# First pair of output tiles of both SwiGLU stages computed from features before the division by the deviation

## What is computed

```
def rms_norm(x, g):
    xf = x.astype(jnp.float32)
    y = xf * lax.rsqrt(jnp.mean(xf * xf, axis=-1, keepdims=True) + EPS)
    return (y * g.astype(jnp.float32)).astype(x.dtype)

def modulate(h, shift, scale):
    return h * (1 + scale) + shift

def swiglu(h, w1, w3, w2):
    return (jax.nn.silu(h @ w1) * (h @ w3)) @ w2

        # first_block, in each of the two layers:
        h = h + g1 * y
        hn = modulate(rms_norm(h, norm_ffn_g[layer]), sh2, sc2)
        h = h + g2 * swiglu(hn, ffn_w1[layer], ffn_w3[layer], ffn_w2[layer])
```

## Time and profile before

| | us |
|---|---|
| three runs, median | 1212.85 |
| three runs, lowest and highest | 1206.35 and 1214.12 |
| span of the profiled execution | 1207.4 |
| TensorE busy in it | 1149.0 (95%) |
| VectorE busy | 814.4 (67%) |
| ScalarE busy | 589.9 (49%) |
| GpSimd busy | 81.8 (7%) |

### The profile page before, as it was taken

How to read it: one execution, slowest core, us unless ns; L and a number is a source line. 1 busy time by engine, 2 the same in 40 slices (tenths; PEclk the granted TensorE clock), 3 DMA queues, 4 the chain that set the end, 5 groups by cost and what they waited for, 6 DMA issues and landing times.

```text
span 1207.4 us, 24317 instructions
## 1 busy us (share of the span) xinstructions
PE 1149.0 (95%) x10429; PEld 1092.4 (90%) x10429; DVE 814.4 (67%) x1490; ACT 589.9 (49%) x1084; POOL 81.8 (7%) x100
## 2 busy tenths in 40 slices
PE   5888789999998999999989999999999999999999
PEld 2687689999997999999989888888999999999999
DVE  3783668898886767555674678787664665877543
ACT  2434556454544545454465557653234445655432
POOL 0000110000011000001100111112600001000000
PEclk9789999999999999999998999999999999999999
DMA  9751548889884555751653232232123464855520
GB/s 388 291 207 60 215 170 329 334 340 349 320 328 174 222 222 223 255 187 43 246 175 105 106 105 80 97 105 71 38 72 106 157 211 159 323 198 185 208 84 14
DMA packets 32363, 226.41 MB, mean 188 GB/s; under 512 B 3584, under 2 KB 4736, under 8 KB 5120
## 3 DMA queue, kind: packets, MB, share of 16 engines
q1 hardware_dynamic: 30528, 221.20, 49.1%
q10 hardware_dynamic: 1728, 3.67, 0.8%
HBM read 223.80 MB, written 1.05 MB: 186 GB/s over the span
## 4 chain that ended last, share of the span: by engine, by line
PE 86%; DVE 8%; ACT 4%; DMA 1%; issue 1%; POOL 0%; SPq 0%; DVEq 0%; POOLq 0%
PE bank L562 23%; PE bank L563 22%; PE bank L564 22%; PE bank L1041 2%; PE bank L687 2%; DVE sb_tmp L1915 1%; DVE sb_ring L1930 1%; DVE sb_wlo L1889 1%; PE bank L580 1%; PE bank L1032 1%; PE bank L1063 1%; DMA sb_ring<-in_ada 1%; PE bank L590 1%; PE bank L600 1%; PE bank L1229 1%; PE bank L1247 1%
## 5 line engine op out<-in xcount | busy, mean ns | idle before, releaser
L562 PE MATMUL bank<-sb_xh,sb_whi 128*128 128x256 f32 x1488 | 422.9, 284 | 9.0 <-DVE sb_wlo L1889 6.7
L563 PE MATMUL bank<-sb_xl,sb_whi 128*128 128x256 f32 x1488 | 414.3, 278 | 0.0
L564 PE MATMUL bank<-sb_xh,sb_wlo 128*128 128x256 f32 x1488 | 414.3, 278 | 0.0
L1889 DVE TENSOR_TENSOR sb_wlo<-sb_ring,sb_whi 128x1024 fp32r<-128x1024 f32 (+1 forms) x197 | 239.1, 1220 | 138.5 <-ACT sb_whi L1375 138.1
L562 PEld LDWEIGHTS bank<-sb_xh,sb_whi 128*128 128x128 f32 x1488 | 281.6, 189 | 17.6 <-issue 12.8
L563 PEld LDWEIGHTS bank<-sb_xl,sb_whi 128*128 128x128 f32 x1488 | 282.2, 190 | 0.1
L564 PEld LDWEIGHTS bank<-sb_xh,sb_wlo 128*128 128x128 f32 x1488 | 281.7, 189 | 0.0
L1375 ACT ACTIVATE sb_whi<-sb_ring 128x1024 fp32r<-128x1024 f32 (+1 forms) x197 | 206.7, 1053 | 88.7 <-PE bank L564 81.3
L1889 DVE TENSOR_TENSOR sb_wlo<-sb_more,sb_whi 128x1024 fp32r<-128x1024 f32 x108 | 131.0, 1222 | 64.8 <-ACT sb_whi L1375 64.8
L562 PE MATMUL bank<-sb_hh,sb_whi 128*128 128x256 f32 x608 | 168.4, 277 | 0.0
L564 PE MATMUL bank<-sb_hh,sb_wlo 128*128 128x256 f32 x608 | 167.8, 276 | 0.0
(11 more groups left out here) (378 smaller groups left out, 1845.6 us busy)
## 6 DMA issues: line engine op xcount, KB each, us to landing
sb_more<-in_w SPq DMA_DIRECT2D x34, 1024.0 KB, 6.7
sb_ring<-in_w SPq DMA_DIRECT2D x32, 1024.0 KB, 6.0
sb_ring<-in_adaT SPq DMA_DIRECT2D x26, 1024.0 KB, 7.6
sb_ring<-in_f SPq DMA_DIRECT2D x22, 1024.0 KB, 5.0
sb_more<-in_adaT SPq DMA_DIRECT2D x18, 1024.0 KB, 9.5
sb_ring<-in_gn SPq DMA_DIRECT2D x8, 1024.0 KB, 4.9
sb_ring<-in_gd SPq DMA_DIRECT2D x8, 1024.0 KB, 4.9
sb_ring<-in_up SPq DMA_DIRECT2D x8, 1024.0 KB, 5.9
```

Of the source, the lines that this page charges most:

```text
L562: te.matmul(out, wh, rh, start=start, stop=False, skip_group_check=skip)
L563: te.matmul(out, wh, rl, start=False, stop=False, skip_group_check=skip)
L564: return te.matmul(out, wl, rh, start=False, stop=stop, skip_group_check=skip)
L1889: ve.tensor_tensor(lo, x, hi.bitcast(F32), ALU.subtract).then_inc(*lo_dve.up(n))
```

## The change

For pair 0 of both layers the product no longer starts from the finished `xh` and `xl`. With r the factor of a token (one over the deviation), the input of SwiGLU is (h times scale) times r plus shift. So the weights' product with it is r times (weights times h times scale), plus weights times shift. `gh` and `gl` hold the high and low parts of h times scale for 256 tokens, and of the shift as columns 257 and 258 (twice the same, which makes the width even). ScalarE writes `gh` behind each square, VectorE writes `gl` behind each residual, one tile later. TensorE's `unnormed` runs pair 0 on them in two banks; the sums of squares stand after feature tile 1 of it, the spreading of the factor after tile 4, and the idle matmuls are left out. Pair 1 then runs as `opening` did before. ScalarE copies the spread factor to SBUF after `upper`, VectorE multiplies both outlets by it and copies out the shift's column, the Silu takes it as bias, and a last operation of VectorE adds the other shift's product and multiplies.

```
-                idle(2)
+                idle(2 * (norm not in ("ffn0", "ffn1")))
...
-                idle(2 * (norm not in ("mix0", "ctx", "fin")))
+                idle(2 * (norm not in ("mix0", "ctx", "fin", "ffn0", "ffn1")))
...
+            def unnormed(layer, norm, outs):
+
+                us = [F.take(f"w13_{layer}")[0] for _ in outs]
+                for u in us:
+                    P.wait_ge(*lo_done(u))
+                P.wait_ge(*dve.at("gl", norm, "shift"))
+                for k in range(KT):
+                    c = slice(k * 128, (k + 1) * 128)
+                    P.wait_ge(*act.at("gh", norm, k))
+                    for u, out in zip(us, outs):
+                        _, hi, lo = unit_of(u)
+                        te.matmul(out, hi[:, c], gh[:, k, :], start=k == 0, stop=False)
+                        te.matmul(out, lo[:, c], gh[:, k, :], start=False, stop=False)
+                    P.wait_ge(*dve.at("gl", norm, k))
+                    for e, (u, out) in enumerate(zip(us, outs)):
+                        _, hi, _ = unit_of(u)
+                        end = te.matmul(out, hi[:, c], gl[:, k, :], start=False, stop=k == KT - 1)
+                        if k == KT - 1:
+                            end.then_inc(*pe.up(("up", layer, 0, e), ("unit", u)))
+                    if k == 1:
+                        mean_square_rest(norm)
+                    if k == 4:
+                        spread(norm)
+                for u in us:
+                    F.done(u)
...
                 for j in range(NH0):
-                    ps = take(RG, ("up", layer, j), (dve, ("prod", layer, j)))
                     if j == 0:
-                        opening(f"w13_{layer}", norm, [(ps[:, 0:T], True), (ps[:, T:2 * T], False)], [("up", layer, 0, e) for e in range(2)])
-                    for e in range(2 if j else 0):
+                        unnormed(layer, norm, [take(RG, ("up0", layer, e), (dve, ("up0", layer, e)))[:, 0:T + 2] for e in range(2)])
+                    else:
+                        ps = take(RG, ("up", layer, j), (dve, ("prod", layer, j)))
+                    if j == 1:
+                        opening(f"w13_{layer}", norm, [(ps[:, 0:T], True), (ps[:, T:2 * T], False)], [("up", layer, 1, e) for e in range(2)])
+                    for e in range(2 if j > 1 else 0):
...
+            def upper_scaled(norm, i, j):
+
+                A.wait_ge(*dve.at("h", norm, j))
+                A.wait_ge(*dve.at("scl", i))
+                sc.activation(gh[:, j, 0:T], h[:, j, :], ACT.Copy, scale=scl[:, i, j:j + 1]).then_inc(*act.up(("gh", norm, j)))
...
                 upper(norm, mods[:, layer, 24:32], xh, free)
+                sc.activation(sq[:, 1, :], ps_of(("spread", norm))[:, 0:T], ACT.Copy).then_inc(*act.up(("R", norm)))
...
+                    if j == 0:
+                        A.wait_ge(*dve.at("up0", layer, 0))
+                        sc.activation(r, sq[:, 2, :], ACT.Silu, bias=st[:, 0:1]).then_inc(*act.up(("silu", layer, j)))
...
+            def lower_scaled(norm, i, j):
+
+                V.wait_ge(*act.at("gh", norm, j))
+                V.wait_ge(*dve.at("h", norm, j))
+                ve.scalar_tensor_tensor(gl[:, j, 0:T], h[:, j, :], scl[:, i, j:j + 1], gh[:, j, 0:T].bitcast(F32),
+                                        ALU.mult, ALU.subtract).then_inc(*dve.up(("gl", norm, j)))
...
             m2 = dve.now()
+            V.wait_ge(*m2)
+            scaled(2, C("nf", 0, 8), mods[:, 0, 32:40])
+            dve.note(("scl", 2))
+            lower_shift(0, "ffn0")
...
                 residual("ffn0", j, "mo", mods[:, 0, 16 + j:17 + j])
+                if j > 0:
+                    lower_scaled("ffn0", 2, j - 1)
                 if j == 6:
                     split(ahead)
+            lower_scaled("ffn0", 2, 7)
...
+                    if j == 0:
+                        V.wait_ge(*act.at("R", norm))
+                        for e in range(2):
+                            ps = ps_of(("up0", layer, e))
+                            V.wait_ge(*pe.at("up", layer, 0, e))
+                            ve.tensor_copy(st[:, e:e + 1], ps[:, T:T + 1]).then_inc(*dve.up())
+                            ve.tensor_tensor(sq[:, 2 + e, :], ps[:, 0:T], sq[:, 1, :], ALU.mult).then_inc(*dve.up(("up0", layer, e)))
+                        V.wait_ge(*dve.now())
+                        V.wait_ge(*act.at("silu", layer, 0))
+                        ve.scalar_tensor_tensor(r, sq[:, 3, :], st[:, 1:2], r, ALU.add, ALU.mult).then_inc(*dve.up(("prod", layer, 0)))
```

46 lines of the change are left out of this document (33 added, 13 removed).

## The result

| | before | changed |
|---|---|---|
| median of 6 runs each, on the same chip, us | 1211.51 | 1221.61 |
| lowest and highest, us | 1206.35 to 1214.85 | 1217.78 to 1222.14 |
| span of the profiled execution, us | 1207.4 | 1218.6 |

The ratio is 1.0099, 95% interval 1.0079 to 1.0119: the change makes the kernel 1.0% slower, 12 us of 1211.5 (9.6 to 14.4). The ratio is the recorded estimate and not the quotient of the medians in the table; those differ by 10.1, which lies inside the interval too. The forecast was 1222, a loss of 9.35, and the change is just at the 1% that was named as what a measurement can tell.

What follows compares the result with a forecast made beforehand. TensorE's chain bounds the kernel, with VectorE's `apply` and two splits setting the pace ahead of pair 1. Terms 0.4 + 2.95 + 1.6 + 2 x 2.2 = 9.35 on 1212.85 give 1222 us, range 1214 to 1230.

Steps and rivals of the forecast that it cites:

- The gap ahead of pair 1: TensorE waits for U2's and U3's `wlo`, split behind `apply`: 7.5 us in layer 0, 7.2 in layer 1.
- The clock: Behind each gap ahead of pair 1, 22 matmuls run at granted clock 0.50, costing 2.2 us a layer.
- the clock stays up: Rival: no half clock behind the gaps ahead of pair 1, so 1218 us; chance 0.12.
- down for all of pair 1: Rival: all of pair 1 runs at half clock, 2 x 2.6 us more, 1227; chance 0.08.
- The rival of 1243: Pair 0's wider matmuls run at the full float32 rate, 20.6 us more; chance 0.05.
- So `wlo` moves from 180.08 to 180.43: Layer 0, ahead of pair 0: one `gh` of 0.35 us on ScalarE delays U1's `wlo`.
- Layer 1: Pair 0 starts at the pooling's end, 389.86; pair 1 ends 1.6 us later, plus 2.2 for the clock.
- The wait ahead of the mixer: Layer 0: two small VectorE operations before `mixout`'s first split add 0.4 us (0.3 to 0.6) to TensorE's 3.12.
- tips over: Rival: the wait ahead of the mixer reaches 3.5, the clock falls, another 2.2 us, 1224.5; chance 0.13.
- The signs that were named: Changed profile: early pair 0, `apply` about 2 us later in layer 0 only, 7 to 8 us gaps, then half clock.
- What costs nothing: `gl` during `mixout`, pair 0's longer outlet and later next units are covered; without that cover 1 to 2 us.
- faster: Rival: both `wlo` come before or inside `apply`, so pair 1 doesn't wait: -9.6 us, 1203; chance 0.05.

Runs made afterwards that it cites:

- e1: Changed kernel with the splits of U2 and U3 moved ahead of `apply` in both layers; 1209.23 us, ratio 1.0010.
- e4: Kernel before, with the splits of U2 and U3 moved ahead of `apply`; 1209.56 us, ratio 1.0005.
- e2: Changed kernel with 14 idle matmuls on TensorE between pair 0 and pair 1 in both layers; 1216.94 us, ratio 1.0062.
- e3: Changed kernel with the small scale and shift operations moved from ahead of the mixer's splits to behind them; 1222.49 us, ratio 1.0094.
- e8: Changed kernel with the spreading behind feature tile 2 of pair 0 in place of tile 4; 1219.43 us, ratio 1.0097.
- e11: Changed kernel with ScalarE writing `gh` of a tile behind the next unit's rounding during `mixout`; 1219.02 us, ratio 1.0083.
- e5: e1 with the spreading behind tile 3 and the small operations moved as in e3; 1207.60 us, ratio 0.9990.
- e7: e5 with pair 0's outlet ahead of the next split and layer 0's adaLN tiles one pair later; 1203.29 us, ratio 0.9959.
- e12: e7 with `gh` written behind the next rounding as in e11; 1203.04 us, ratio 0.9938.

## Why the prediction held, point by point

The time (1222 forecast, 1221.61 measured) and the range held. The median of before was 1211.5 in the runs beside it and not 1212.85, so the loss was 12 (9.6 to 14.4; 10.1 between the medians) where I had 9.35. The hit to 0.4 us is luck in part: a base that was 1.3 too high made up for a loss that was too small. What was missing from my sum are two paces, 1.6 to 1.8 us in layer 0 and 1.2 in layer 1, both below; 9.35 and 2.9 make about 12.3. The two stages of the profiles lose 14.0, more than that, since the profile of before happens to have the full clock at the mixer's start and behind the wait for `z`, where the changed kernel's has half clock at both (about 0.8 each).

**The gap ahead of pair 1** is the heart of it, and it held to a tenth: 7.20 us for 7.5 in layer 0 and 6.88 for 7.2 in layer 1, both ended by a `wlo`. From the spreading to `apply` I had 0.65, and the rows have 187.33 - 186.68 = 0.65; from `apply` to pair 1 I had 9.3, and they have 196.63 - 187.33 = 9.30. e1 took the two splits out from behind `apply`, and the loss of 1% was gone; e4 showed that the same edit is worth nothing in the kernel before. This cause is shown.

**The clock** behind the gaps was 2.2 a layer in my sum; e2 measured 2.25 and 2.24. At 0.50 ran 24 matmuls in layer 0 and 21 in layer 1, against 22 behind the gap of 4.55. An estimate from the 6, 11 or 14 slow matmuls of the Trainium skill (TensorE: Matmul & The Clock Gate, section "What's actually happening") would have been 0.6 to 1.4; here the measurement decides, and it goes with this kernel's own row. The rivals "the clock stays up" and "down for all of pair 1" fall: the clock was down behind all eight gaps of over 5 us in the profiles (changed, e3, e8, e11), and back before pair 1 ended.

**The width of 258 and the float32 rate**: behind the first matmul of pair 0, which takes 0.20 to the next (0.19 and 0.22 for the first ones of pair 0 and of the mixer before, at 256 columns), the rows are 0.12 apart (398.39, 398.51 and 398.62 above), so pair 0 ran at the pitch of 256 columns. The rival of 1243 falls.

**Layer 0, the step that was too small.** I had 2.95 + 2.2 = 5.15 from the mixer's first matmul to the end of pair 1, and it was 8.2. Of the 3.1 that are missing, 2.5 lie ahead of pair 0. The step that failed is "So `wlo` moves from 180.08 to 180.43": I counted one `gh` of 0.35 ahead of U1's rounding, as though the other seven ran beside something, and only asked whether VectorE had room in TensorE's tile of 2.8 us. But the turn of the two engines was 3.05, longer than the tile already, so each added 0.40 made every turn longer. e11 shows 1.6 to 1.8 for that. The other 0.8 is the half clock at the mixer's start. Pair 0 up to the spreading took 4.58 for 4.25, and pair 1 7.99 for 7.8; these make up the rest.

**Layer 1** was 3.8 and came out at 5.8. The step that failed is that pair 0 starts when the pooling would have ended before: the pooling, in which TensorE had set the pace, is now paced by VectorE. VectorE's timeline has, first before and then in the changed kernel:

```profile
387.32 0.48 DVE L1944 SCALAR_TENSOR_TENSOR sb_h<-bank,sb_gcol,sb_h 128x256 f32<-128x256 f32 x1 [0.38 <-PE bank L905]
```
```profile
395.69 0.47 DVE L1996 SCALAR_TENSOR_TENSOR sb_h<-bank,sb_gcol,sb_h 128x256 f32<-128x256 f32 x1
396.08 0.56 DVE L2111 SCALAR_TENSOR_TENSOR sb_gl<-sb_h,sb_scl,sb_gh 128x256 fp32r<-128x256 f32 x1
```

Before, VectorE waited 0.38 for TensorE ahead of each residual; now it goes from residual to `gl` without a wait, and TensorE waits 0.85 for a residual ahead of pair 0. The residuals start 0.95 apart (393.75 to 398.50 is five) where they were 0.865 apart before, 386.45 to 389.91 being four. From the matmul behind the wait for `z` to pair 0 it takes 12.45 in three profiles at the full clock (e2, e5, e7) where the earlier trace rows give 389.86 - 378.60 = 11.26: 1.2 more, which I put down to VectorE's pace by these rows; no run here changes that pace by itself. It takes 13.3 in the changed kernel: 0.8 more for the half clock at 386.2. `apply` behind it kept its distances.

**The wait ahead of the mixer** grew from 3.12 to 3.42, 0.3 for 0.4. The rival "tips over" is right in that this execution has a stretch of half clock there, and wrong in its cause: e3 took the 0.3 away and the stretch stayed, and kernels with 3.12 and with 3.41 have been seen with it and without. I had reasoned from one wait of 3.12 in one execution that a wait of that length leaves the clock alone. It costs 0.8 to 1.3 there and not the rival's 2.2. What decides it remains open; nothing here was aimed at it.

**The signs that were named**: the gaps, what ended them, the half clock behind them and the place of the two splits are there. Two signs are not. Pair 0's first matmul was to come about 1 us after the mixer's last and came behind a wait of 2.44; and `apply` was to start no later in layer 1, but it starts 18.5 behind the wait for `z` (403.41 - 384.90) where it started 16.55 behind it before (395.15 - 378.60). Most of both is the two paces again.

**What costs nothing** held in the changed kernel, for TensorE had no wait in pairs 2 to 4. I had put 1 to 2 us on the loss of that cover, and e1, in which the gap is gone, shows 1.55 for the outlet in each layer and 1.67 for the next unit in layer 0.

**The rival "faster"** had its condition right (both `wlo` there by the end of `apply`) and its price too high. With the condition met by e1 pair 1 ends 1.2 and 2.8 us earlier than before, not 4.4 and 5.6, since the turns of the mixer and the pace of the pooling had already made `apply` later, and 1.55 to 3.2 of it is given back in pair 2. It takes e12 (split first, outlet first, adaLN tile later, `gh` behind the rounding, and e5's two moves) to get 7.5 us (4.4 to 10.5) of the 9.6.
